# One decoder step on one core: attention order tables made anew, and work moved across five stage borders

## The reference, cut to what matters

```python
h = rms_norm(xp, g_mix[l])
qd, kd, vd, qs, ks_, vs = project(h, w_in[l])        # one 1024 x 3072 product
# 1024 new tokens, blocks of 128 queries; 8 sample sequences of 8 new tokens over 2048 cached keys
od = diff_attention(...)            # 4 heads of 2 x 64: softmax(0) - lam * softmax(1), then a norm per head
osb = stick_breaking_attention(...) # 8 heads of 64: products of sigmoids, strictly causal
xp = xp + concat([od, osb]) @ w_out[l]
xp = xp + hmoe(rms_norm(xp, g_ffn[l]), ...)          # top 1 of 4 groups, top 2 of 4 experts, SwiGLU 1024-256-1024
y = rms_norm(xp, g_final)
```

## Time and profile before

| | us |
|---|---|
| time, median of 3 runs (lowest, highest) | 1415.95 (1415.18, 1416.37) |
| the profiled execution: time | 1414.32 |
| the profiled execution: span, first to last instruction | 1412.5 |
| TensorE busy, of the span | 1265.7 (90%) |
| DVE, ACT, POOL busy | 795.3, 660.1, 154.6 |
| mean granted TensorE clock | 0.949 of full |

### The profile page before, as it was taken

One profiled execution on the slowest core, in us unless ns is written; L12 is line 12 of the kernel. 1 busy time (PEld: TensorE's weight loads), 2 busy tenths in 40 slices (PEclk: granted clock), 3 DMA queues, 4 the chain that ended last, 5 costly groups with the idle time before them and its releaser, 6 DMA issues. The chain is left out here.

```text
span 1412.5 us, 26208 instructions
## 1 busy us (share of the span) xinstructions
PE 1265.7 (90%) x8895; PEld 953.0 (67%) x8895; DVE 795.3 (56%) x1118; ACT 660.1 (47%) x1086; POOL 154.6 (11%) x175
## 2 busy tenths in 40 slices
PE   7999999998999999569999996999299999999930
PEld 6878888887776776357767765887176766667610
DVE  4322112200877777358889995443666565666627
ACT  5520223001677677346676774232255555656512
POOL 0100000000110111100000000000112232222036
PEclk9999999999999999879999998999599999999975
DMA  6622423145989799489897874542689986532187
GB/s 201 221 87 79 130 97 127 56 155 185 348 271 350 250 373 315 170 270 372 283 354 271 301 270 127 179 164 90 247 288 376 406 349 239 179 113 97 72 314 260
DMA packets 159645, 319.15 MB, mean 226 GB/s; under 512 B 21815, under 2 KB 50906, under 8 KB 155418
## 3 DMA queue, kind: packets, MB, share of 16 engines
q1 hardware_dynamic: 146666, 274.48, 55.4%
q0 software_dynamic: 7200, 26.22, 5.5%
q10 hardware_dynamic: 5648, 16.78, 3.0%
HBM read 318.79 MB, written 55.77 MB: 265 GB/s over the span
## 5 line engine op out<-in xcount | busy, mean ns | idle before, releaser
L2368 DVE TENSOR_TENSOR w_gate_up_split<-w_gate_up,w_gate_up_split 128x2048 fp32r<-128x2048 f32 x64 | 143.8, 2288 | 109.1 <-ACT w_gate_up_split L2417 108.4
L2319 PE MATMUL gate_up_ps<-w_gate_up_split,slot_rows_T 128*128 128x512 f32 x768 | 185.8, 398 | 4.2 <-DVE slot_rows_T L2376 4.1
L327 PE MATMUL proj_ps<-w_in_split,x_T_hi 128*128 128x512 f32 x576 | 183.4, 395 | 0.0
L2319 PEld LDWEIGHTS gate_up_ps<-w_gate_up_split,slot_rows_T 128*128 128x128 f32 x768 | 143.2, 190 | 39.4 <-DVE slot_rows_T L2376 10.3
L1149 PE MATMUL turns_and_scores_ps<-ident,pages 128*128 128x128 f32 (+1 forms) x1088 | 132.6, 275 | 6.7 <-DVE q_by_block L1405 4.9
L1149 PEld LDWEIGHTS turns_and_scores_ps<-ident,pages 128*128 128x128 f32 (+1 forms) x1088 | 120.6, 144 | 20.9 <-issue 20.1
L2417 ACT ACTIVATE w_gate_up_split<-w_gate_up 128x2048 fp32r x62 | 115.3, 1908 | 33.7 <-issue 33.7
L461 ACT ACTIVATE proj_rows<-proj_ps,sum_squares 128x512 f32<-128x512 f32 x36 | 24.8, 690 | 224.3 <-PE proj_ps L327 219.7
L327 PEld LDWEIGHTS proj_ps<-w_in_split,x_T_hi 128*128 128x128 f32 x576 | 108.9, 189 | 22.6
L2341 PE MATMUL expert_out_ps<-w_down,expert_act_T 128*128 x256 | 115.3, 593 | 1.3 <-ACT expert_out L2447 1.3
L1683 PE MATMUL mix_out_ps<-w_out_split,oT_split 128*128 128x512 f32 x432 | 105.0, 400 | 10.4 <-DVE oT_split L1745 10.4
(11 more groups left out here) (231 smaller groups left out, 1962.2 us busy)
## 6 DMA issues: line engine op xcount, KB each, us to landing
pages<-in_cache_s SPq DMA_DIRECT2D x256, 256.0 KB, 5.2
pages<-in_cache_d SPq DMA_DIRECT2D x226, 256.0 KB, 5.1
w_gate_up<-in_w_gate SPq DMA_DIRECT2D x34, 1024.0 KB, 8.5
w_gate_up<-in_w_up SPq DMA_DIRECT2D x34, 1024.0 KB, 10.2
w_down<-in_w_down SPq DMA_DIRECT2D x34, 1024.0 KB, 12.3
scratch_moe_out<-expert_out ACTq DMA_DIRECT2D x32, 512.0 KB, 3.9
w_in_now<-in_w_in SPq DMA_DIRECT2D x48, 256.0 KB, 2.9
pages_ahead<-in_cache_d SPq DMA_DIRECT2D x30, 256.0 KB, 3.5
```

What stands on the lines that cost most here:

```text
L327: last = pe.matmul(pj_ps[:, n % PJ_BANKS, :], h[:, k, at], w[g % 2][:, k, :], start=(k == 0 and m == 0), stop=(k == KC - 1 and m == 2))
L2319: last = pe.matmul(gu_ps[:, u, :], xT[:, u, a, k, :], gu_split[:, u, b, k, :], start=(k == 0 and m == 0), stop=(k == KC - 1 and m == 2))
L2368: dve.tensor_tensor(gu_split[:, u, 1, at, :].rearrange("p k (c n) -> p k c n", c=2), raw[:, at, :, :], gu_split[:, u, 0, at, :].bitcast(F3 ...
```

## The change

1. `ORDERS` has new strings for PE, DVE and ACT in both kinds. The counts of all letters are as before; DVE has a new letter, `b`, four times in each kind. In DIFF the fourth `z` now stands behind the last `a`. In STICK the third and the fourth `z` stand last.
2. The waits on project's six store semaphores stand at the head of SP's stream in DIFF (`t.proj_stores`) and no longer at project's end.
3. `b` (`spread`) on DVE holds what stood ahead of the loop and in `page(it, 0)`: in turn 0 the memset of `q_block`, and in DIFF the wait for `q_in` and its 16 copies; in each turn the two copies into `q_block`. TensorE no longer waits for `zeroed` at a stage's start.
4. STICK's `z` of turns 2 and 3 does nothing: these outputs stay in `head_oT`, which `mix_out` reads as its last two blocks (`parts_of_o`). SP's stream in STICK ends with a wait for the three older stores and with the loads of output tiles 0 and 1, now of 6 blocks out of 8 (`load_oT`, `oT_tiles`).
5. In `mix_out`, `high_o(0)` and `low_o(0)` stand ahead of the 8 slices of `w_out`, and each split of a tile is two instructions, of 6 and 2 blocks.
6. The gather of slot rows 0 is issued by GpSimd at the end of `route`, as soon as `slot_tok` is written, and no longer at the start of `experts`.

```diff
-        "PE": ("ppppsqssqpospppooqqsppppooqqsotopppppqqqtossspppsoqppussptooaaaqqtppppoouaaaaaqqsstoopptootpssaqaaoo"
...
-               "aaasstootpsspppofqqoupzpppuootsstoqqaaatsoppotpospaasotqoppoosssaaaaqaqatouopppoosstootqqaaaaaasszzs"
-               "sotufuuoaaaaooaaaaaaaatototaaaoaatft"),
...
+        "PE": ("ppppppqssqsqpospppooqqsppppqsooppotpqqqpoppotpssussoaaaaqqppppotosstootaaqqspppotuosspoostoqaaaotsst"
...
+               "aaaatoossssootaaaaaptotppuqsopppuufqqsooppptotopsooaaaaaqqqppppssootaaaaaaqqssstooppaaaaqaaptooqsssso"
+               "uufotaaautooaaaaazaaaootaatotaaaaztf"),
...
-        "DVE": ("ppppsmsmmmsmmmsppppmmmkskkppppmmnkstnmppppkkqqqqqqqqqktppkkwmmssnmpssppkmmmssntppmmtkmppppnmmuusmsnm"
...
+        "DVE": ("ppppbppsmsmmmskmmmsppppmmmkksppnppsmmmppkktkqqqqqqqqqbkkknwppptppnssmmmssmmmpppptnmmtssntnmskkkppmmm"
...
 # STICK
...
-        "PE": ("ssppoppqoqppposoqqppppqppoqquppppussaaaaqqaspoppuaaqqoppppossqaaqoosppasoooppssuoqaaaaqpooppoaqaspop"
...
-               "saaaaaoooaaaaaozoofo"),
...
+        "PE": ("psspppqqoppsoqpppoqqppppuoqqqppppoqqpppuusssoaaaaaaaqqppppoqqppppssoqqoopasspooossaaqaaoupoopppaaaaaq"
...
+               "aaaaoooaaaaaaooofozz"),
...
@@ SP, end of project; start and end of attention
-                for u in range(3):
-                    sp.wait_ge(rows_stored[u], 16 * len(range(u, len(in_rows), 3)))
-                    sp.wait_ge(qkT_stored[u], 16 * len(range(u, len(staged), 3)))
...
                 if kind == DIFF:
+                    for stored, stores in t.proj_stores:
+                        sp.wait_ge(stored, stores)
                     sp.dma_start(q_in[:, :, :], t.qT[:, :, SEQ:SEQ + N_SAMPLE]).then_inc(q_in_loaded, 16)
...
                 def store(it):
                     if kind == DIFF:
                         kept(sp, "turn_out", it, PT - 1)
+                    elif it >= TURNS - 2:
+                        return
...
                     for u in range(2):
-                        sp.wait_ge(oT_stored[u], 16 * TURNS)
+                        sp.wait_ge(oT_stored[u], 16 * (TURNS - 1))
+                    for n in range(O_PLACES):
+                        load_oT(sp, t, n)
...
@@ TensorE and VectorE in attention
-                pe.wait_ge(zeroed, 1)
...
+                def spread(it):
+                    if it == 0:
+                        dve.memset(q_block[:, :, :, :], 0.0).then_inc(zeroed, 1)
+                        if kind == DIFF:
+
+                            dve.wait_ge(q_in_loaded, 16)
+                            for u in range(2):
+                                for s in range(DEC_BATCH):
+                                    dve.tensor_copy(t.q_heads[half(u), s, :, u, :], q_in[half(u), :, DEC_SEQ * s:DEC_SEQ * (s + 1)])\
+                                       .then_inc(zeroed, 1)
+                            dve.wait_ge(zeroed, 1 + 2 * DEC_BATCH)
+                        else:
+                            dve.memset(s_left[:, KEYS:KEYS + 1], 1.0).then_inc(zeroed, 1)
+                            dve.wait_ge(zeroed, 3)
+                    dve.wait_ge(ps_done.sem, ps_done.after(it, -1))
+                    for odd in range(2):
+                        dve.tensor_copy(q_block[:, :, odd::2, 16 * odd:16 * odd + 16],
...
@@ mix_out
+def load_oT(sp, t, n):
+    sp.dma_start(t.oT_tiles[:, n % O_PLACES, :, :], t.oT[:, 0:FAR_BLOCKS, n * P:(n + 1) * P])\
+      .then_inc(t.oT_loaded[n % O_PLACES], 16)
...
+        def parts_of_o(n):
+            far, near = slice(0, FAR_BLOCKS), slice(FAR_BLOCKS, BLOCKS)
+            if n == LAST:
+                return (far, s_oT[:, far, :]), (near, s_oT[:, near, :])
+            return (far, t.oT_tiles[:, n % O_PLACES, :, :]), (near, t.head_oT[:, :, n * P:(n + 1) * P])
...
+                low_o(0)
                 for k in range(BLOCKS):
-                    if k == 2:
-                        low_o(0)
...
+                high_o(0)
                 for k in range(BLOCKS):
-                    if k == 2:
-                        high_o(0)
...
@@ GpSimd, end of route, start of experts
+                pool.wait_ge(step, t.n_slot_tok)
+                gather_rows(pool, t, 0)
...
-                for tile in range(ROW_PLACES):
+                for tile in range(1, ROW_PLACES):
                     gather_rows(pool, t, tile)
```

More of the change, by code:

```diff
@@ L501, in _ @@
                         tables.exps_of_sums(act)
+        t.proj_stores = [(sem, 16 * len(range(u, len(n), 3))) for n, of in ((in_rows, rows_stored), (staged, qkT_stored))
+                         for u, sem in enumerate(of)]
         t.left = sems
@@ L765, in steps_of @@
         apply=[(it, s) for it in firsts for s in range(D_PAGES)],
+        spread=[(it,) for it in firsts],
         rows=[(it,) for it in firsts],
@@ L1401, in _ @@
                 steps = dict(score=score, soft=soft_diff if kind == DIFF else soft_stick, out=out, turn_out=turn_out, norm=norm,
-                             page=page, page_scores=page_scores, weigh=weigh_diff if kind == DIFF else weigh_stick,
+                             spread=spread, page=page, page_scores=page_scores, weigh=weigh_diff if kind == DIFF else weigh_stick,
                              turn=turn, rows=rows, heads=heads)
                 steps |= dict(share=share) if kind == STICK else dict(peak=peak)
-                dve.memset(q_block[:, :, :, :], 0.0).then_inc(zeroed, 1)
-                if kind == DIFF:
-                    dve.wait_ge(q_in_loaded, 16)
-                    for u in range(2):
-                        for s in range(DEC_BATCH):
-                            dve.tensor_copy(t.q_heads[half(u), s, :, u, :], q_in[half(u), :, DEC_SEQ * s:DEC_SEQ * (s + 1)])\
-                               .then_inc(zeroed, 1)
-                    dve.wait_ge(zeroed, 1 + 2 * DEC_BATCH)
-                else:
+                if kind == STICK:
                     dve.memset(left[:, :, :, SEQ:SEQ + 1], 1.0).then_inc(zeroed, 1)
-                    dve.memset(s_left[:, KEYS:KEYS + 1], 1.0).then_inc(zeroed, 1)
-                    dve.wait_ge(zeroed, 3)
+                    dve.wait_ge(zeroed, 1)
                 for name, *args in orders["DVE"]:
@@ L1606, in mix_out @@
         x_loaded = [sem(f"x_again_loaded{u}") for u in range(2)]
-        o_loaded = [sem(f"oT_loaded{u}") for u in range(O_PLACES)]
         x1_stored, h_stored = t.x1_stored, t.h_stored
@@ L1656, in _ @@
                 load_x(1)
-                for n in range(2, O_PLACES):
-                    load_o(n)
                 load_route_constants(sp, t)
@@ L1870, in high_o @@
                         act.wait_ge(y_done, 2 * (n - 2) + 2)
-                    src = oT[:, n % O_PLACES, :, :] if n < LAST else s_oT[:, :, :]
-                    act.activation(oT_split[:, n % 2, 0, :, :], src, ACT.Copy).then_inc(o_hi, 1)
+                    for blocks, src in parts_of_o(n):
+                        act.activation(oT_split[:, n % 2, 0, blocks, :], src, ACT.Copy).then_inc(o_hi, 1)
                 def square_sum(n):
```

81 lines of the change are left out of this document (40 added, 41 removed).

## The result

The changed kernel takes 1393.99 us (median of 4 runs, 1390.57 to 1398.68), the kernel before 1415.57 in the same comparison (4 runs, 1413.1 to 1416.37): a ratio of 0.9855, 95% interval 0.9833 to 0.9876. It is faster, as forecast, but by 21.6 us and not by 31.6, and 1393.99 lies at the upper edge of the range. Later the unaltered kernel was run once more and gave 1391.24 (5 runs, 1390.9 to 1394.94; ratio 0.9845, 0.9831 to 0.9859).

What follows compares the result with a forecast made beforehand. TensorE was taken to pace both attention stages, leaving time to gain at stage borders. Gains of 1.8 + 21.4 + 4.4 + 4.0 = 31.6 us off 1414.3, with 1.6 for the median, gave 1384; range 1377 to 1395.

Steps and rivals of the forecast that it cites:

- Border DIFF to STICK: TensorE's pause before STICK: 3.6 us instead of 25.03, a gain of 21.4, bounds 19.4 to 23.6.
- SP's demand: End of DIFF: 17 pages x 2 x 0.63 = 21.4, with two `z` at 0.35 together 22.1 us.
- The 2.0: DIFF to STICK: SP ends 2.0 us after TensorE, taken between 3.7 (0.63 an issue) and 0.4 (0.33).
- The 1.6: DIFF to STICK: from SP's end to TensorE's start some 1.6 us without `zeroed`, 1.95 before.
- SP's backlog stays: Rival at DIFF's end: 8 pages unissued at the third `z`, 9 behind it; pause 12.9, time 1393 us; chance 0.08.
- Border project to DIFF: DIFF's start: store wait off project's end, TensorE starts some 2 us earlier; gain 1.8 us, bounds 0 to 3.8.
- Border STICK to mix_out: Store and load leave the chain, VectorE's slices set the pace: gain 4.4 us, bounds 3.0 to 5.6.
- the sign for it: mix_out's first product comes 5.5 to 6 us behind VectorE's last copy, not 10.4, waiting for VectorE's slices.
- Border route to experts: Gather issued in route, rows 4.4 us earlier, then VectorE's splits late: gain 4.0 us, bounds 1.0 to 4.4.
- The lock: End of route: gather could block a VectorE instruction through their shared port pair, 0.9 us; gain 3.1 not 4.0, time 1385.
- Orders at 0: New instruction orders: worth 0, between a gain of 2.4 us and a loss of 5.
- That rival: DMA becomes the bound of DIFF, as 8.4 MB more move in the stage: slower, 1428 us at 265 GB/s; chance 0.03.

Runs made afterwards that it cites:

- the repeat: The changed kernel run again with nothing altered: 1391.24 us, ratio 0.9845 to the kernel before.

## Why the prediction was wrong

**Border DIFF to STICK: the step that failed is SP's demand.** The prediction let SP start on STICK's pages 0.5 us after the first of the 17 `a`, priced the issues at 0.63 only if DMA was saturated and at 0.33 otherwise, and took SP to end 2.0 us after TensorE. The start held: SP had waited for the first `a` and issued STICK's first page 0.76 us after that `a` began (570.46 against 569.70). The price did not: 0.33 is the DMA instruction alone, and the rest of SP's program for a load was left out, so that price never applied to cached pages in a row, whatever their bytes. The 2.0 was chosen between 3.7, by the dearer price, and 0.4, and both were too low. From 570.46 to the end of the last store are 24.9 us, where the dearer price gave 22.1, and TensorE needs 17.4 for the same stretch: 7.5 us behind, at 0.72 and 0.68 an issue. What goes beyond 0.63 lies in 0.9 us of waits and in some longer instructions (up to 946 ns for an issue and 867 for a read of page numbers); why these were longer is not shown. With the 1.95 from SP's end to TensorE that is the pause of 9.4. The 1.6 that was taken for the way from SP's end without the wait on `zeroed` stayed 1.95. Gain 15.6 and not 21.4, below the lower bound of 19.4. The rival "SP's backlog stays" was nearest to the mechanism, at 0.08: SP came to the third `z` at about 581.6, when TensorE's run of `a` around it had ended at 577.69; its pause of 12.9 was too long, since the 18 issues behind the third `z` took 12.16 us, but 5.2 of that still lay beside TensorE.

**Border project to DIFF.** TensorE's earlier start came about as worked out (3.17 us after project's end, 2.8 forecast), and so did `q` (VectorE done at 357.1, 356.6 forecast). The step that failed is the reckoning of what `q` and two `s` behind it are worth: the copy of pages that the next step waits for was not in it (1.30), and the first score moved from 10.8 to 14.3 us after project's end. Without the second fall of the clock, pause and DIFF take 240.0 to 240.6 us in four profiles with this start, and 240.5 and 240.0 in the two of kernels with the start of before, so the border gained nothing that shows, and not 1.8; in the first profiled execution the fall turned it into a loss of 2.1. The bound below, 0, was too high for that.

**Border STICK to mix_out** was right, with the chain named: 4.8 against 4.4, the pacing by VectorE's slices included. Only the sign for it was off: the first product came 4.0 us behind VectorE's last copy, not 5.5 to 6, since it needs only the first slice.

**Border route to experts.** The chain had a link that wasn't seen: the end of a block waits for GpSimd's queue to drain, and with a gather just issued this takes 4.6 us; in the earlier trace rows no gather was under way there. VectorE's weight split, taken to begin 4.0 us after `slot_tok` as in the earlier trace rows, began 5.9 after it. So the first product came 2.4 sooner and not 4.0. The second link was the clock: the first group of products ended only 0.9 sooner than without the early gather, and at the end 1.0 was left in the first profile and 0.3 in the repeat. The lower bound of 1.0 was just met in one and missed in the other. The lock of the page "SBUF — State Buffer" in the Trainium skill, section "SBUF: two separate sides", did not show: the five VectorE instructions that began while the gather's row ran (990.20 to 991.35) took 0.17 to 0.18 us each, as the same five did without it. That section limits the lock to VectorE instructions in a two-port mode, or with two inputs in SBUF against a GpSimd instruction that reads SBUF, which the prediction left out; three of the five have two inputs.

**The rest.** Orders at 0 was off the other way: STICK got 1.3 to 1.6 us shorter. DMA did not become the bound of DIFF: its share was 0.89 from 360 to 560 us, with 306 GB/s. That rival's 417 GB/s for the pause of before was a rate of issue; by the windows view of the trace the chip moved 324 there, at a DMA share of 0.93, and from 565 to 585 us, most of which it took as empty, 99.

Of the 11.5 us that the profiled execution is short of the sum, 5.8 lie at DIFF to STICK, 3.9 at project to DIFF and 3.0 at route to experts, against 1.6 that STICK and mix_out gave more; 0.5 is project's, 0.1 rounding. What stays open is how much of the 0.63 to 0.72 us would go if the page numbers were read elsewhere or earlier.

## What to carry to other kernels

When a wait is taken away from a queue that works in order, count what the queue still has to do, by the spacing of its rows when they come in a row and from the moment at which it is free; here that spacing was 0.63 to 0.72 us while the DMA instruction alone is listed at 0.33, because each load also needs its page number and its address. Work that can wait should not be pulled ahead of a border only because the engine that issues it seems idle: leaving half of the prefetches to the next stage was worth 6 to 9 us more. A transfer that is issued just ahead of a stage's end may be waited for by all engines, and TensorE, started earlier but then idle for 3.93 us, mostly ran its next products at the lower clock for longer.

## What was not expected of the hardware

- SP's page loads of 64 KB came as slowly as those of 256 KB: 0.64 to 0.69 us apart against 0.68 to 0.72, with the DMA share at 0.56 and 1.01. About half of that is the DMA instruction; the rest is SP's work on page numbers and addresses, and the spaces between instructions.
- At the end of a block GpSimd's drain took 4602 ns with an indirect DMA just issued; in the kernel before, with none, 48 ns:

```profile
L2040 POOLq DRAIN  x1: 48/48/48, 992.8 to 992.8; - x1
```

- The same program fell to 0.52 and 0.62 of the clock in 358 to 366 us in one profiled execution and stayed at 1.00 in the other, with waits of the same length ahead of it. It cost 2.6 us, and a fall like it shows in three of seven profiles with that start.
